# A two-block transformer kernel: the 16 meta tokens' transposes and products cut from 128 to 16 rows and columns, and their memsets removed

## The chip, the core and the metric

The kernel runs on one core of a Trainium2 chip. The core has TensorE (PE, with its weight loads shown apart as PEld), VectorE (DVE), ScalarE (ACT), GpSimd (POOL) and SyncE (SP), which starts DMAs. The engines run side by side and wait for each other through semaphores. The time is that of one execution on the device in microseconds (us); lower is better.

## The reference

Two transformer blocks in float32 are run one after the other, on 512 tokens of width 1024. The first puts 16 learned meta tokens in front (528 tokens) and has two layers: one with differential attention (here stage A) and one with latent attention (stage B), each followed by a gated MLP with a short convolution. The second block has a convolution and windowed attention side by side (stage C) and another MLP. The change touches the attention of the first block alone:

```python
# differential attention (A), 8 heads: q1, q2, k1, k2 64 wide, v 128 wide, L = 528 keys
a = softmax(mask(q1 @ k1.T * 64**-0.5)) - lam * softmax(mask(q2 @ k2.T * 64**-0.5))
o = a @ v
# latent attention (B), 16 heads: q and k 96 wide (64 + 32 rotary), v 64 wide
p = softmax(mask(q @ k.T * 96**-0.5))
o = p @ v
# mask: key chunk <= query chunk; the 16 meta tokens are chunk 0, then chunks of 64
```

## The kernel before, in words

Activations lie with features on the 128 partitions and tokens along the free axis. Weights come in halves of 128 x 1024. ACT makes a rounded copy `w_hi` of each (L1383), POOL the rest `w_lo` (L434), and every linear product is three passes: `w_hi` with `x_hi`, `w_hi` with `x_lo`, `w_lo` with `x_hi` (L455 to L457). The products inside the attention are plain float32.

Each head's queries are done in five units, from the longest to the shortest. A unit `idx` has `t = 4 - idx` blocks of 128 keys behind the 16 meta keys: units 0 to 3 have 128 queries and 16 + 128 t keys, unit 4 has the 16 meta queries and the 16 meta keys (`nq` = 16, t = 0). For a unit the engines do this:

- PE `scores` (L577): queries x keys into PSUM. In A two maps from 64 rows each, on partitions 0 to 63 and 64 to 127; in B one map from 96 rows.
- DVE `maximum` (L997, L999), ACT `exps` (L1473), DVE `combine` (L1010 to L1021): the probabilities in `prob`, queries on partitions, keys along the free axis, the meta keys in columns 0 to 15.
- PE `transposes`: t blocks of 128 keys (L596), then the block that holds the meta keys (L600). L600 transposes columns 0 to 127 of `prob`, of which the first 16 are wanted.
- ACT `take_transposed`: copies the t blocks to `pt` (L1483) and rows 0 to 15 of the meta block to `pt_meta` (L1485).
- PE `values`: t products with `v_tok` (L614) and one with `v_meta` (L616), summed in one PSUM region; stationary are the values (128 wide in A, 64 in B), moving the probabilities. DVE `take_output` (L1028) copies the result away.

`value_transposes` does once per head what `transposes` does for the values: four blocks (L634) and the meta block (L635); ACT copies them (L1491, L1493).

L616 multiplies all 128 rows of `v_meta` and `pt_meta`, of which ACT fills 16. So at the start POOL clears `v_meta`, `pt_meta` and `prob` (L438 to L440) and raises `blocks_clear`, for which PE waits once, ahead of the first value transposes, and ACT once, ahead of the first exponentials.

All orders are written out by hand. In A (`head_a` on PE) a head runs, for each unit: scores of the next unit, transposes of this one, a piece of the next head's projections (24 products in three passes; in unit 3 a second piece follows the values), values of this one; then the next head's value transposes. In B (`head_b`): pieces 0 and 1 of the next head, values 4 of the head before, scores 2, transposes 0, scores 3, piece 2, transposes 1, values 0, scores 4, piece 3, value transposes, values 1, transposes 2, next head's scores 0, values 2, transposes 3, next head's scores 1, values 3, transposes 4. Semaphores count up from unit to unit; PE waits for `a_ready` (combined probabilities), `pt_ready` (ACT's copies), `exp_done`, `qk_ready` (rotated queries and keys) and `o_taken`.

In the built program each product names the part of the 128 x 128 array it takes, rows (contraction) x columns (width of the stationary operand), rounded up to 32, 64 or 128: 64x128 for A's scores, 128x64 for B's values, 128x128 for all else in A and B, B's 96-row scores among it.

Of the kernel before, what the change touches and what calls it, by code (L numbers as in the profile page):

```python
# [31 lines left out]
P = 128  # L32
D = 1024
KD = D // P
META = 16
# [124 lines left out]
def wait(eng, semaphore, value):  # L160

    if not isinstance(value, int) or value > 0:
        eng.wait_ge(semaphore, value)


def program(nc, x_t, stream, params, positions, out):
    tabs_dram = nc.inline_tensor(rotary_tables(), "rotary_tables").ap()
    consts_dram = nc.inline_tensor(shape_constants(), "shape_constants").ap()
    with ExitStack() as ctx:
# [3 lines left out]
        def sem(name):  # L173
            return ctx.enter_context(nc.semaphore(name))
# [20 lines left out]
        ident = cst[:, 0:P]  # L195
        at = [0]

        def carve(n):
            at[0] += n
            assert at[0] <= SCRATCH  # L200
            return scratch[:, at[0] - n:at[0]]
# [4 lines left out]
        vt_buf = carve(T1)  # L206
        v_tok = carve(2 * 512).rearrange("p (a n) -> p a n", a=2)
        v_meta = carve(2 * P).rearrange("p (a n) -> p a n", a=2)
        o_buf = carve(KD * T1).rearrange("p (k t) -> p k t", k=KD)
        prob = carve(4 * T1).rearrange("p (a m t) -> p a m t", a=2, m=2)  # L210
        pt = carve(2 * 512).rearrange("p (a n) -> p a n", a=2)
        pt_meta = carve(2 * P).rearrange("p (a n) -> p a n", a=2)
# [65 lines left out]
        ps = ctx.enter_context(nc.psum_tensor("ps", [P, 8, 512], F32))  # L278
# [24 lines left out]
        g_ready = sem("g_ready")  # L303
        consts_set = sem("consts_set")
        lam_step = sem("lam_step")
        blocks_clear = sem("blocks_clear")
        lam_exp_done = sem("lam_exp_done")
        tabs_made = sem("tabs_made")
        rot_step = sem("rot_step")
# [1 line left out]
        vt_done = sem("vt_done")  # L311
# [70 lines left out]
        def unit(idx):  # L382
            t = 4 - idx
            nq = P if t else META
            return t, nq, (META + P * (t - 1) if t else 0)
# [11 lines left out]
        def prob_of(slot):  # L397
            return prob[:, slot // 2, slot % 2, :]
# [4 lines left out]
        @block.sync  # L403
        def _(sp):
            def load_half(j, i=0):

                wait(sp, lo_ready, j - 3 + 4 * i)
                sp.dma_start(w_raw[:, j % 4, :], stream[j + 4 * i]).then_inc(raw_loaded[j % 4], 16)

            for j in range(4):  # L410
                sp.dma_start(h[:, 2 * j:2 * j + 2, :], x_t[:, 2 * j:2 * j + 2, :]).then_inc(x_loaded[j], 16)
                if j == 0:
                    load_half(0)
            for j in range(1, 4):
                load_half(j)
            with sp.Fori(0, HALVES // 4 - 1) as i:
                for j in range(4, 8):
                    load_half(j, i)
            for j in range(HALVES // 4 * 4, HALVES):
                load_half(j)  # L420
            for m in range(KD):
                sp.wait_ge(fin_ready, m + 1)
                sp.dma_start(out[:, m, :], h[:, m, META:T1]).then_inc(stored, 16)
            sp.wait_ge(stored, 16 * KD)


        @block.gpsimd
        def _(pool):
            def lo_part(j, i=0):
                pool.wait_ge(hi_ready, j + 1 + 4 * i)  # L430
                wait(pool, half_done, j - 3 + 4 * i)
                for c in range(0, HW, HW // LO_CUTS):
                    cols = slice(c, c + HW // LO_CUTS)
                    last = nc.gpsimd.tensor_tensor(w_lo[:, j % 4, cols], w_raw[:, j % 4, cols],  # L434
                                                   w_hi[:, j % 4, cols].bitcast(F32), ALU.subtract)
                last.then_inc(lo_ready, 1)

            nc.gpsimd.memset(v_meta[:, :, :], 0.0)  # L438
            nc.gpsimd.memset(pt_meta[:, :, :], 0.0)
            nc.gpsimd.memset(prob[:, :, :, :], 0.0).then_inc(blocks_clear, 1)  # L440
            for j in range(4):
                lo_part(j)
            with pool.Fori(0, HALVES // 4 - 1) as i:
                for j in range(4, 8):
                    lo_part(j, i)
            for j in range(HALVES // 4 * 4, HALVES):
                lo_part(j)
# [3 lines left out]
        def _(pe):  # L451
# [129 lines left out]
            def transposes(kind, hd, turn, idx, more=True):  # L581

                t, nq, _ = unit(idx)
                u = (5 * hd if kind == "A" else 5 * HEADS_A + 5 * hd) + idx
                pb = prob_of(prob_slot(kind, turn, idx))
                pe.wait_ge(a_ready, u + 1)
                wait(pe, pt_ready, u)
                if kind == "A" and idx == 0:
                    pe.wait_ge(v_ready, hd + 1)
                    wait(pe, o_taken, u)  # L590
                if kind == "B" and idx == 0 and more:
                    pe.wait_ge(kv_taken, 2 * hd + 3)
                if kind == "B" and idx == 2 and more:
                    pe.wait_ge(v_ready, HEADS_A + hd + 2)
                for b in range(t):
                    last = nc.tensor.transpose(ps[:, 6, b * P:b * P + nq],  # L596
                                               pb[0:nq, META + b * P:META + b * P + P], ident[0:nq, 0:nq])
                bank, c = (6, t * P) if t < 4 else (7, 0) if kind == "A" else (1, 384)

                last = nc.tensor.transpose(ps[:, bank, c:c + P], pb[:, 0:P], ident)  # L600
                last.then_inc(t_done, 1)

            def values(kind, hd, turn, idx):

                t, nq, _ = unit(idx)
                u = (5 * hd if kind == "A" else 5 * HEADS_A + 5 * hd) + idx
                up, par_ = (turn + idx) % 2, turn % 2
                pe.wait_ge(pt_ready, u + 1)
                wait(pe, o_taken, u)
                w = P if kind == "A" else 64  # L610
                rows = slice(0, P) if kind == "A" else slice(64 * par_, 64 * par_ + 64)
                o = ps[rows, 7, P:P + nq]
                for b in range(t):
                    nc.tensor.matmul(o, v_tok[:, par_, b * w:b * w + w], pt[:, up, b * P:b * P + nq],  # L614
                                     start=b == 0, stop=False)
                nc.tensor.matmul(o, v_meta[:, par_, 0:w], pt_meta[:, up, 0:nq],  # L616
                                 start=t == 0, stop=True).then_inc(pv_done, 1)

            def value_transposes(kind, hd, par_):

                if kind == "A":
                    pe.wait_ge(chunk_taken, 6 * hd + 6)
                    wait(pe, pt_ready, 5 * hd)
                    wait(pe, o_taken, 5 * hd)
                    meta = ps[:, 7, 0:P]
                else:
                    pe.wait_ge(kv_taken, 2 * hd + 2)
                    if not isinstance(hd, int) or hd:
                        pe.wait_ge(pt_ready, 5 * HEADS_A + 5 * hd - 3)
                    pe.wait_ge(chunk_taken, 6 * HEADS_A + 2 * hd + 1)  # L630
                    meta = ps[:, 0, 384:512]

                for b in range(4):
                    nc.tensor.transpose(ps[:, 6, b * P:b * P + P], vt_buf[:, META + b * P:META + b * P + P], ident)  # L634
                nc.tensor.transpose(meta, vt_buf[:, 0:P], ident).then_inc(vt_done, 1)  # L635

            def sub_sum(n, bank0):

# [58 lines left out]
            for p in range(6):  # L697
                piece_a(0, p)
            scores("A", 0, 0, 0)
            pe.wait_ge(blocks_clear, 1)  # L700
            value_transposes("A", 0, 0)
            head_a(0, 0)
            with pe.Fori(0, (HEADS_A - 2) // 2) as i:
# [38 lines left out]
            for m in range(TILES_C):  # L742
# [4 lines left out]
                if m == 4:  # L747
                    pe.wait_ge(y_ready, 3)
                    for b in range(4):
                        last = nc.tensor.transpose(ps[:, 3, b * P:b * P + P], vt2[:, b * P:b * P + P], ident)  # L750
                    last.then_inc(vt2_done, 1)
                for u in range(8):
# [3 lines left out]
                    if m == s_at + 2:  # L756
                        pe.wait_ge(p2_ready, u + 1)
                        wait(pe, pt2_ready, u)
                        for i in range(4):
                            for kb in range(k0 // P, 2):  # L760
                                last = nc.tensor.transpose(ps[:, 6 + kb, i * P:i * P + P],
                                                           prob2[:, i, kb * P:kb * P + P], ident)
                        last.then_inc(t2_done, 1)
                    if m == s_at + 4:
# [3 lines left out]
                        for kb in range(k0 // P, 2):  # L768
                            last = nc.tensor.matmul(ps[0:64, 1, :], v2[:, n - 1 + kb, g * 64:g * 64 + 64],  # L769
                                                    pt2[:, kb, :], start=kb == k0 // P, stop=kb == 1)  # L770
                        last.then_inc(pv2_done, 1)
                for u in range(8):
                    g, n = divmod(u, 4)
                    k0 = 0 if n else P
                    if m == unit2_at(u):
                        pe.wait_ge(k2q2_ready, 6)
                        wait(pe, masked, u)
                        for i in range(4):
                            e, pair = divmod(i, 2)
                            rows = slice(64 * e, 64 * e + 64)  # L780
                            last = nc.tensor.matmul(ps[:, 4 + e, pair * 256 + k0:pair * 256 + 256],
                                                    q2[rows, 2 * g + pair, n * P:n * P + P],
                                                    k2[rows, g, (n - 1) * P + k0:(n + 1) * P],
                                                    start=True, stop=True)
# [581 lines left out]
        def _(act):  # L1366
# [198 lines left out]
            inverse_rms(N_A, D, T1, r)  # L1565
            for j in range(3, 7):
                hi_part(j)
            act.wait_ge(blocks_clear, 1)
            exps("A", 0, 0, 0)
            take_values("A", 0, 0)  # L1570
            head_a(0, 0, 4)
# [47 lines left out]
            for m in range(TILES_C):  # L1619
# [4 lines left out]
                for u in range(8):  # L1624
# [5 lines left out]
                    if m == unit2_at(u) + 1:  # L1630
                        k0 = 0 if u % 4 else P
                        act.wait_ge(max2_step, 4 * u + 4)
                        for i in range(4):
                            last = A.activation(prob2[:, i, k0:], prob2[:, i, k0:], ACT.Exp, bias=neg2[:, i:i + 1],
                                                accum_out=sum2[:, i:i + 1])
# [150 lines left out]
```

## Time and profile before

| | us |
|---|---|
| median of three runs | 2223.09 |
| lowest, highest run | 2222.1, 2229.47 |
| the profiled execution, time | 2229.47 |
| the profiled execution, span of the core | 2227.3 |

The profile is of one execution. The page gives busy times by engine, the chain of waits that ended last, and groups of instructions by line. A plain float32 product shows as two instructions with a load each, a transpose and a pass of L455 to L457 as one. Matmul rows overlap, because their ends are modelled with a tail: the distance between two starts tells more than a duration. In a row of the timeline the stationary shape (rows*columns) stands ahead of the moving one. A is the stretch up to about 270 us, B that from 768 to 1000 us; between them and behind them stand the MLPs and stage C.

### The profile page before, as it was taken

Reading aid. Unit: us, or ns where it says so; the run is one execution under the profiler, and the core shown is the slowest. Engines: PE = TensorE matmul, PEld = TensorE weight load, DVE = VectorE, ACT = ScalarE, POOL = GpSimd, SP = SyncE. Lnnn points to the kernel's source line nnn. Section 1 sums busy time; section 2 is a strip of 40 time slices with the busy share of each in tenths; the row PEclk is TensorE's granted clock in tenths of the full one; section 3 lists DMA queues with packets and bytes.
Section 4 is the critical chain, followed back from the end, with each engine's and each line's share of the span. In section 5 each row is a group of like instructions: output and inputs, shape, how many; then the busy total and the mean of one; then the engine's idle time right before and its main releaser. Section 6 shows DMA issues by size and latency. Waiting matters only on the chain.

```text
span 2227.3 us, 40390 instructions
## 1 busy us (share of the span) xinstructions
PE 2150.4 (97%) x14044; PEld 1907.1 (86%) x14044; DVE 1138.0 (51%) x2068; ACT 786.1 (35%) x1407; POOL 1113.8 (50%) x1387
## 2 busy tenths in 40 slices
PE   7999899999999899999999999999999999999997
PEld 7888799999999777769999999877778878888886
DVE  6666745334146777763544414775631364425244
ACT  3444524222133355542422313434343224323232
POOL 5444246545556421113655546664455575656553
PEclk9999999999999999989999999999999999999999
DMA  4222122222223201112222222322222232322322
GB/s 172 72 71 75 57 67 98 92 85 94 95 76 114 67 31 36 38 34 76 94 95 85 94 95 86 103 85 76 85 85 95 97 120 86 104 85 94 104 85 76
DMA packets 52502, 188.25 MB, mean 85 GB/s; under 512 B 5824, under 2 KB 5952, under 8 KB 52416
## 3 DMA queue, kind: packets, MB, share of 16 engines
q1 hardware_dynamic: 51408, 185.16, 24.7%
q10 hardware_dynamic: 1008, 1.89, 0.3%
q8 instruction: 60, 0.98, 0.2%
q14 instruction: 26, 0.21, 0.0%
HBM read 184.93 MB, written 2.10 MB: 84 GB/s over the span
## 4 chain that ended last, share of the span: by engine, by line
PE 88%; DVE 8%; ACT 2%; issue 2%; DMA 0%; DVEq 0%; SPq 0%; ACTq 0%
PE ps L455 27%; PE ps L457 26%; PE ps L456 26%; PE ps L577 3%; PE ps L614 2%; PE ps L596 1%; DVE g_lo L822 1%; PE ps L616 1%; DVE g_hi L820 1%; PE ps L769 1%; ACT scratch L1473 1%; PE ps L600 1%; DVE scratch L942 1%; DVE scratch L1021 0%; ACT scratch L1529 0%
## 5 line engine op out<-in xcount | busy, mean ns | idle before, releaser
L434 POOL TENSOR_TENSOR w_lo<-w_raw,w_hi 128x256 fp32r<-128x256 f32 x1380 | 1111.2, 838 | 1088.8 <-ACT w_hi L1383 1088.8
L455 PE MATMUL ps<-x_hi,w_hi 128*128 128x264 f32 (+2 forms) x2760 | 881.2, 319 | 3.9 <-DVE scratch L1348 2.4
L456 PE MATMUL ps<-x_lo,w_hi 128*128 128x264 f32 (+2 forms) x2760 | 868.6, 315 | 0.0
L457 PE MATMUL ps<-x_hi,w_lo 128*128 128x264 f32 (+2 forms) x2760 | 867.5, 314 | 0.0
L455 PEld LDWEIGHTS ps<-x_hi,w_hi 128*128 128x128 f32 x2760 | 522.9, 189 | 47.6 <-issue 7.7
L456 PEld LDWEIGHTS ps<-x_lo,w_hi 128*128 128x128 f32 x2760 | 521.5, 189 | 33.1 <-issue 0.8
L457 PEld LDWEIGHTS ps<-x_hi,w_lo 128*128 128x128 f32 x2760 | 521.5, 189 | 32.3
L1383 ACT ACTIVATE w_hi<-w_raw 128x1024 fp32r<-128x1024 f32 x345 | 361.3, 1051 | 314.5 <-PE ps L457 311.9
L455 PE MATMUL ps<-g_hi,w_hi 128*128 128x264 f32 (+2 forms) x1312 | 409.2, 312 | 15.3 <-DVE g_lo L822 14.5
L456 PE MATMUL ps<-g_lo,w_hi 128*128 128x264 f32 (+2 forms) x1312 | 408.0, 311 | 0.0
L457 PE MATMUL ps<-g_hi,w_lo 128*128 128x264 f32 (+2 forms) x1312 | 407.4, 311 | 0.0
L455 PEld LDWEIGHTS ps<-g_hi,w_hi 128*128 128x128 f32 x1312 | 249.5, 190 | 32.0 <-DVE g_lo L822 17.1
L456 PEld LDWEIGHTS ps<-g_lo,w_hi 128*128 128x128 f32 x1312 | 249.6, 190 | 13.1
L457 PEld LDWEIGHTS ps<-g_hi,w_lo 128*128 128x128 f32 x1312 | 249.6, 190 | 13.0
L833 DVE TENSOR_TENSOR h<-ps,h 128x528 f32 (+2 forms) x80 | 55.9, 699 | 287.4 <-PE ps L457 287.4
L1442 ACT ACTIVATE scratch<-scratch,par 128x528 f32<-128x528 f32 (+2 forms) x66 | 54.3, 822 | 321.3 <-DVE scratch L848 321.3
L848 DVE TENSOR_TENSOR scratch<-ps,r 128x528 f32<-128x528 f32 (+2 forms) x66 | 46.1, 698 | 152.1 <-PE ps L457 136.2
L1473 ACT ACTIVATE scratch<-ps,small 128x400 f32<-128x400 f32 (+4 forms) x160 | 76.6, 481 | 105.5 <-DVE small L999 104.5
L858 DVE TENSOR_TENSOR scratch<-ps,r 128x528 f32<-128x528 f32 (+2 forms) x66 | 46.1, 698 | 129.7 <-PE ps L457 129.7
L577 PE MATMUL ps<-scratch 64*128 64x16 f32 (+9 forms) x384 | 94.0, 419 | 15.5 <-DVE scratch L942 7.2
L822 DVE TENSOR_TENSOR g_lo<-scratch,g_hi 128x528 f32 (+6 forms) x98 | 95.4, 974 | 9.7
L1320 DVE TENSOR_TENSOR scratch<-ps,acc 128x512 f32<-128x512 f32 x47 | 32.4, 690 | 130.4 <-PE ps L457 130.3
(169 smaller groups left out, 1760.0 us busy)
## 6 DMA issues: line engine op xcount, KB each, us to landing
w_raw<-stream SPq DMA_DIRECT2D x345, 512.0 KB, 3.2
h<-x_t SPq DMA_DIRECT2D x4, 528.0 KB, 8.6
out_t<-h SPq DMA_DIRECT2D x8, 256.0 KB, 2.1
scratch<-rotary_tables ACTq DMA_DIRECT2D x4, 264.0 KB, 5.6
par<-params ACTq DMA_DIRECT2D x1, 342.5 KB, 5.2
scratch<-positions ACTq DMA_DIRECT2D x1, 256.0 KB, 2.7
cst<-shape_constants ACTq DMA_DIRECT2D x1, 193.0 KB, 6.6
```

Source lines behind the costliest of these rows:

```text
L434: last = nc.gpsimd.tensor_tensor(w_lo[:, j % 4, cols], w_raw[:, j % 4, cols], w_hi[:, j % 4, cols].bitcast(F32), ALU.subtract)
L455: nc.tensor.matmul(out_ap, w_hi[:, s, c], xh[:, k, cols], start=first, stop=False)
L456: nc.tensor.matmul(out_ap, w_hi[:, s, c], xl[:, k, cols], start=False, stop=False)
L457: return nc.tensor.matmul(out_ap, w_lo[:, s, c], xh[:, k, cols], start=False, stop=last)
L577: last = nc.tensor.matmul(flat[:, b + k0:b + k1], q, k_buf[rows, turn % 2, k0:k1], start=True, stop=True)
L822: V.tensor_tensor(lo, src, hi.bitcast(F32), ALU.subtract).then_inc(ready, 1)
L833: V.tensor_tensor(hm, result(j + m, T), hm, ALU.add).then_inc(tile_taken, 1)
L848: V.tensor_tensor(cut(a_pad[:, 2:2 + T], T), result(j, T), cut(r[:, 0:T], T), ALU.mult).then_inc(tile_taken, 1)
L858: V.tensor_tensor(cut(b_val[:, 0:T], T), result(j + 1, T), cut(r[:, 0:T], T), ALU.mult).then_inc(tile_taken, 1)
L1383: A.activation(w_hi[:, j % 4, :], w_raw[:, j % 4, :], ACT.Copy).then_inc(hi_ready, 1)
L1442: A.activation(conv[:, 0:T], a_pad[:, 0:T], ACT.Identity, bias=par[:, bass.ds(b + 2 * i, 1)], scale=par[:, bass.ds(o + 2 * i, 1)]).then_in ...
L1473: last = A.activation(prob_of(c)[0:nq, 0:nk], flat[0:nq, b:b + nk], ACT.Exp, bias=neg_max[0:nq, c:c + 1], accum_out=sums[0:nq, c:c + 1])
```

## The change

The meta transposes take 16 columns in place of 128 and write 16 partitions; the meta products contract over 16 rows in place of 128. With that nothing reads the rows that the memsets cleared, and they go, with their semaphore and the two waits for it. All other instructions and their order stay.

```diff
--- before.py
+++ after.py
@@ -303,7 +303,6 @@
         g_ready = sem("g_ready")
         consts_set = sem("consts_set")
         lam_step = sem("lam_step")
-        blocks_clear = sem("blocks_clear")
         lam_exp_done = sem("lam_exp_done")
         tabs_made = sem("tabs_made")
         rot_step = sem("rot_step")
@@ -435,9 +434,6 @@
                                                    w_hi[:, j % 4, cols].bitcast(F32), ALU.subtract)
                 last.then_inc(lo_ready, 1)
 
-            nc.gpsimd.memset(v_meta[:, :, :], 0.0)
-            nc.gpsimd.memset(pt_meta[:, :, :], 0.0)
-            nc.gpsimd.memset(prob[:, :, :, :], 0.0).then_inc(blocks_clear, 1)
             for j in range(4):
                 lo_part(j)
             with pool.Fori(0, HALVES // 4 - 1) as i:
@@ -597,7 +593,7 @@
                                                pb[0:nq, META + b * P:META + b * P + P], ident[0:nq, 0:nq])
                 bank, c = (6, t * P) if t < 4 else (7, 0) if kind == "A" else (1, 384)
 
-                last = nc.tensor.transpose(ps[:, bank, c:c + P], pb[:, 0:P], ident)
+                last = nc.tensor.transpose(ps[0:META, bank, c:c + P], pb[:, 0:META], ident)
                 last.then_inc(t_done, 1)
 
             def values(kind, hd, turn, idx):
@@ -613,7 +609,7 @@
                 for b in range(t):
                     nc.tensor.matmul(o, v_tok[:, par_, b * w:b * w + w], pt[:, up, b * P:b * P + nq],
                                      start=b == 0, stop=False)
-                nc.tensor.matmul(o, v_meta[:, par_, 0:w], pt_meta[:, up, 0:nq],
+                nc.tensor.matmul(o, v_meta[0:META, par_, 0:w], pt_meta[0:META, up, 0:nq],
                                  start=t == 0, stop=True).then_inc(pv_done, 1)
 
             def value_transposes(kind, hd, par_):
@@ -622,17 +618,17 @@
                     pe.wait_ge(chunk_taken, 6 * hd + 6)
                     wait(pe, pt_ready, 5 * hd)
                     wait(pe, o_taken, 5 * hd)
-                    meta = ps[:, 7, 0:P]
+                    meta = ps[0:META, 7, 0:P]
                 else:
                     pe.wait_ge(kv_taken, 2 * hd + 2)
                     if not isinstance(hd, int) or hd:
                         pe.wait_ge(pt_ready, 5 * HEADS_A + 5 * hd - 3)
                     pe.wait_ge(chunk_taken, 6 * HEADS_A + 2 * hd + 1)
-                    meta = ps[:, 0, 384:512]
+                    meta = ps[0:META, 0, 384:512]
 
                 for b in range(4):
                     nc.tensor.transpose(ps[:, 6, b * P:b * P + P], vt_buf[:, META + b * P:META + b * P + P], ident)
-                nc.tensor.transpose(meta, vt_buf[:, 0:P], ident).then_inc(vt_done, 1)
+                nc.tensor.transpose(meta, vt_buf[:, 0:META], ident).then_inc(vt_done, 1)
 
             def sub_sum(n, bank0):
 
@@ -697,7 +693,6 @@
             for p in range(6):
                 piece_a(0, p)
             scores("A", 0, 0, 0)
-            pe.wait_ge(blocks_clear, 1)
             value_transposes("A", 0, 0)
             head_a(0, 0)
             with pe.Fori(0, (HEADS_A - 2) // 2) as i:
@@ -1565,7 +1560,6 @@
             inverse_rms(N_A, D, T1, r)
             for j in range(3, 7):
                 hi_part(j)
-            act.wait_ge(blocks_clear, 1)
             exps("A", 0, 0, 0)
             take_values("A", 0, 0)
             head_a(0, 0, 4)
```

The order of PE's instructions is the same in both. In B, unit 1's transposes, unit 0's values and unit 4's scores stand so before (the shape is that of the output; `ps` is PSUM, `cst` holds the identity, `scratch` the probabilities, values, queries and keys):

```order
L596 MATMUL ps<-cst,scratch 128x128 x3
L600 MATMUL ps<-cst,scratch 128x128
L614 MATMUL ps<-scratch 64x128 x4
L616 MATMUL ps<-scratch 64x128
L163 REGISTER_ALU
L577 MATMUL ps<-scratch 128x16
```

and so now:

```order
L592 MATMUL ps<-cst,scratch 128x128 x3
L596 MATMUL ps<-cst,scratch 16x128
L610 MATMUL ps<-scratch 64x128 x4
L612 MATMUL ps<-scratch 64x128
L163 REGISTER_ALU
L573 MATMUL ps<-scratch 128x16
```

Nothing has moved; the lines of the file are shifted by 4, so that L596, L600, L614, L616 and L577 are now L592, L596, L610, L612 and L573, and the meta transpose writes 16 partitions in place of 128. What the output's shape doesn't show: the stationary operand of the meta transpose is now 128x16 (before 128x128), and the meta product contracts 16 rows. The built program gives the meta transposes the part 128x32 of the array, and the meta products 32x128 in A and 32x64 in B.

## Rows read from the trace of the kernel before

**Rows 1.** The page: its first line, and busy time (share) and instructions of each engine

```profile
span 2227.3 us, 40390 instructions
...
PE 2150.4 (97%) x14044; PEld 1907.1 (86%) x14044; DVE 1138.0 (51%) x2068; ACT 786.1 (35%) x1407; POOL 1113.8 (50%) x1387
```

**Rows 2.** The page's chain of waits, shares of the span by engine

```profile
PE 88%; DVE 8%; ACT 2%; issue 2%; DMA 0%; DVEq 0%; SPq 0%; ACTq 0%
```

**Rows 3.** All instructions of L600 and L635: duration ns min/median/max, starts, shapes

```profile
L600 PE MATMUL ps<-cst,scratch x120: 272/273/477, 43.8 to 997.7; 128*128 128x128 f32 x120
...
L635 PE MATMUL ps<-cst,scratch x24: 272/273/273, 38.4 to 976.9; 128*128 128x128 f32 x24
```

**Rows 4.** Stretches from:to: length, busy PE, PEld, DVE, ACT, POOL, clock, DMA

```profile
124.00:152.00 28.00, 26.95 (x214) 24.43 (x213) 19.03 (x52) 11.89 (x35) 12.22 (x16) 1.00 0.23 76
236.00:275.00 39.00, 28.62 (x181) 22.79 (x181) 30.82 (x65) 24.61 (x58) 10.01 (x11) 0.97 0.16 53
840.00:854.00 14.00, 13.30 (x91) 10.27 (x90) 9.90 (x33) 7.46 (x26) 3.04 (x4) 1.00 0.12 38
```

**Rows 5.** PE in order of time in B: start us, us to the last end, line, stationary shape

```profile
857.65 0.49 PE L596 MATMUL ps<-cst,scratch 128*128 128x128 f32 x3
857.97 0.27 PE L600 MATMUL ps<-cst,scratch 128*128 128x128 f32 x1
858.18 1.09 PE L614 MATMUL ps<-scratch 128*64 128x128 f32 x8
859.10 0.38 PE L616 MATMUL ps<-scratch 128*64 128x128 f32 x2
859.41 0.40 PE L577 MATMUL ps<-scratch 96*128 96x16 f32 x2
```

**Rows 6.** PEld (weight loads) in the same stretch

```profile
857.87 0.14 PEld L600 LDWEIGHTS ps<-cst,scratch 128*128 128x128 f32 x1
858.17 0.85 PEld L614 LDWEIGHTS ps<-scratch 128*64 128x64 f32 x8 [0.17 <-issue]
...
859.41 0.30 PEld L577 LDWEIGHTS ps<-scratch 96*128 96x128 f32 x2 [0.17 <-issue]
```

**Rows 7.** PE in order of time in A

```profile
106.74 0.39 PE L616 MATMUL ps<-scratch 128*128 128x128 f32 x2
107.06 0.73 PE L577 MATMUL ps<-scratch 64*128 64x272 f32 x4
```

**Rows 8.** PE in order of time in B: 96 rows behind 128

```profile
851.31 0.27 PE L600 MATMUL ps<-cst,scratch 128*128 128x128 f32 x1
851.42 0.84 PE L577 MATMUL ps<-scratch 96*128 96x400 f32 x2
```

**Rows 9.** POOL in order of time at the start

```profile
1.24 1.86 POOL L440 MEMSET scratch<- 128x2112 f32 x1
8.78 0.93 POOL L434 TENSOR_TENSOR w_lo<-w_raw,w_hi 128x256 fp32r<-128x256 f32 x1 [5.68 <-ACT w_hi L1383]
```

**Rows 10.** What PE waited for in five heads of A: us, times, longest us

```profile
PE ps L634 <- DVE scratch L1028: 2.8, 5, 0.6
PE ps L596 <- DVE scratch L1021: 2.4, 5, 0.5
```

**Rows 11.** PE in order of time in B: two scores that wait

```profile
855.71 0.27 PE L600 MATMUL ps<-cst,scratch 128*128 128x128 f32 x1
856.21 0.51 PE L577 MATMUL ps<-scratch 96*128 96x144 f32 x2 [0.23 <-ACT scratch L1473]
...
862.76 0.27 PE L600 MATMUL ps<-cst,scratch 128*128 128x128 f32 x1
863.51 0.92 PE L577 MATMUL ps<-scratch 96*128 96x16 f32 x3 [0.47 <-DVE scratch L942]
```

**Rows 12.** What PE waited for in fourteen heads of B

```profile
PE ps L577 <- DVE scratch L942: 6.8, 14, 0.7
PE ps L577 <- ACT scratch L1473: 3.0, 13, 0.2
```

## The prediction

> **What bounds the kernel now.** I read the page's busy times first: TensorE is busy for 97% of the span, every other engine for about half [rows 1]. The chain of waits says the same, 88% of it is PE [rows 2]. The memsets of part one of the change are on another engine, so the next question was where the edited TensorE lines run. L600 (the 120 transposes of the 16 meta-token columns) runs from 43.8 to 997.7 us, L635 (its twin for the values, 24 times) from 38.4 to 976.9 [rows 3]. That is two stages: attention A, 8 heads of about 28 us up to 270 us, and attention B, 16 heads of about 14.5 us from 768 to 1000 us. In a steady 28 us of A the matmul rows are busy for 26.95, in 14 us of B for 13.30; in the last A head it is 28.62 of 39 [rows 4]. So time added on TensorE in these stages mostly lands in the total, except where TensorE already waits for somebody. Last I read single rows, since a busy matmul row includes a tail: what counts is the distance from one start to the next.
>
> **What a small product costs.** In B, the transposes L596 (three) start at 857.65 and L600 at 857.97: 0.11 us each [rows 5]. All stream 128 columns, and the weights of L600 load at 857.87, under the last L596 [rows 6]: hidden. Then come products whose stationary operand is 64 columns wide (128*64). The load for the first starts at 858.17, 0.20 us after L600 started where 0.11 is normal [rows 5, 6]. The eight L614 lie 0.109 apart and L616 starts at 859.10, so the first really streams from 859.10 - 8 x 0.109 = 858.23: its load of 0.055 lay open. Leaving that shape costs the same: the second L616 starts 0.11 after the first, at 859.21, and the load of L577 at 859.41, 0.20 again [rows 5, 6]. That load is a plain 128-wide one; the second follows 0.11 later (0.30 for two of 0.19) though only 16 columns stream between them, so it costs 0.11 when open. A shows it for rows: L616 (128*128) twice from 106.74, the second at 106.85, then L577 with 64*128 at 107.06, 0.21 later [rows 7]. Against this, 96 rows after 128 cost nothing: L600 at 851.31, L577 (96*128) at 851.42 [rows 8]; the built program gives both the whole array. My reading: when the part of the array that a product takes changes between whole and half (64 rows or 64 columns), the earlier product runs out first (0.09 us) and the next load lies open: 0.055 for a transpose or 64 columns, 0.11 for 128 plain columns. Sum 0.15 or 0.20 per change of shape.
>
> The Trainium skill, "TensorEngine Tiling (Array Packing)", section "Key Properties", says that changing the tiling mode, not just the tile, drains TensorE; the rows above agree, with their 0.09 us. The same rule speaks against this change.
>
> **The change part by part.** (1) The three memsets and both waits for them. The large one ends at 1.24 + 1.86 = 3.10 us and POOL's first real work starts at 8.78, released by ACT [rows 9]. Worth nothing; the cover is 5.7 us of idle POOL.
>
> (2) The meta transposes L600 and L635: the stationary operand shrinks from 128*128 to 128*16, the moving one stays the 128-column identity. So each still streams for 0.11. The weight load gets shorter, but it is hidden except in the fifth unit of a head, where it comes right behind another shape (0.055 down to an estimated 0.01, so -0.05). The built program gives it a part of the array of 128*32, different from its neighbours', so there is a change of shape on entry and on exit. (3) The meta products L616: 16 rows in place of 128, same columns, so the same stream; part of the array 32*128 (A) or 32*64 (B) where its neighbour L614 has 128*128 or 128*64. One new change on entry; the exit to L577 (A) or L596 (B) was one already.
>
> No row shows a part narrower than 64. Bounds of one such change from the nearest rows: nothing, as 96 against 128 [rows 8], and 0.20 as in [rows 5 to 7]. I take the upper: the half-array rows are the nearer kind. For a load of 16 columns I take 0.01, between 0 and 0.055.
>
> Steady head of A (order: scores, transposes, projection piece, values, five times): enter L600 four times from L596, 4 x 0.10; leave it to a piece five times, 5 x 0.20 = 1.00; enter L616 five times, 1.00; in the fourth unit leave L616 to another piece, 0.20; enter L635, 0.10; fifth L600, -0.05. Sum 2.65. TensorE waits 0.5 us a head for the copy of the fifth output (L1028) ahead of L634, and 0.5 for the combined probabilities (L1021) ahead of L596 [rows 10]. The first wait hides the exit from the fifth L616 (0.15, left out of the sum); the second hides the 0.10 of L635. 2.55 x 7 = 17.9. In the last head TensorE waits anyway [rows 4]: half, 1.2. A: +19.
>
> Steady head of B. Unit 0: L600 in and out to scores, 0.30. But L600 starts at 855.71 and the scores only at 856.21, behind ACT's exponentials, 0.50 where 0.11 is needed [rows 11]: the 0.39 of slack takes it all. Unit 1: L600 in, 0.10 (its exit was a change before); L614 to L616, 0.15. Then L635 0.10, unit 2's L616 is later, unit 1's L616 0.15, unit 2's L600 in and out 0.30: these lie ahead of the next head's first scores, which wait for DVE's rotation from 862.76 + 0.11 to 863.51, 0.64 us [rows 11]; of the 0.55, all is hidden. Left on the path: unit 1's L600 0.10, three L616 (units 0, 2, 3) 0.45, unit 3's L600 0.10 + 0.20, and the fifth unit's L600 -0.05 on entry, +0.20 on exit. Sum 1.00. Both waits recur in every head (14 and 13 times in 14 heads) [rows 12]. 15 heads and a bit: +15.5.
>
> Behind the later transposes stand ACT's copies (L1483, L1485) and behind them the values; the slack there is the score products between, and it does not shrink as long as the delay sits on TensorE itself. DVE is idle for about 30% of both stages and ACT for about half [rows 4], so they follow.
>
> Sum: 19 + 15.5 = 34.5. The profiled execution took 2229.5 (span 2227.3); it would come to 2264. It is the slowest of three, the median is 2223.1, so the forecast is 2223.1 + 34.5 = 2257.6, said as 2258.
>
> **Rivals.** (a) *No waits absorb, or new ones arise.* Without absorption A is 2.8 x 8 = 22.4 and B 1.85 x 16 = 29.6, together 52: 2275. For it: B hands work round between three engines, and a unit that comes later from TensorE delays DVE's next step. Against it: both waits in [rows 11] start from events ahead of the inserted time.
>
> (b) *The narrow transposes stop being transposes.* The transpose is one instruction per block while a plain float32 product is two (L614: eight for four blocks) [rows 5]. If L600 and L635 became plain products, 144 x 0.11 = 16 us more, less what the waits hide (three in each head of B, one in each of A, 56 x 0.11 = 6 us): 34.5 + 10, 2268. The Trainium skill, same page, section "Restrictions", says that column tiling excludes transpose mode for float32 input. No row of before has a transpose on part of the array, so the trace can't tell.
>
> (c) *Only one of the two kinds costs.* The cost may come from rows alone (L616: A 1.2 x 8, B 0.45 x 15, together 16 us, 2239) or from columns alone (the other 18 us, 2241).
>
> (d) *Not slower: no change of shape costs anything* below half the array, because the narrow part lies inside the part its neighbour uses. Then only the shorter open loads remain, 24 fifth units x 0.05 = 1.2 us: 2222. It decides at each exit from L600: if the next load starts 0.11 after L600 it holds. For it: 96 inside 128 [rows 8]. Against it: 64 inside 128 costs 0.09 each way, in every head [rows 5 to 7].
>
> **How the numbers follow.** Forecast with its errors (a change 0.17 to 0.22, absorption a third off) 2247 to 2268: 0.55. (a) 0.13, (b) 0.12, (c) 0.09, (d) 0.08, and 0.03 for something that makes it faster. The range reaches from (c)'s lower case to just past (a): 2238 to 2278, which leaves out (d) and the faster remainder. 0.3%, about what a measurement of this kernel can tell from no change, is 6.7 us: (a), (b), (c) and the forecast are slower, 0.89; (d) is the same, 0.08.
>
> **What will show it.** In the changed profile, in both stages: the next load after an L600 at 0.20 from its start rather than 0.11; L614 to L616 0.20 plus the open load; B's slots behind the fourth L616 0.15 longer. A steady head of A gets 2.5 us longer, one of B 1.0 us (seen from one L635 to the next); waits of L577 in B shrink to near zero. The stages behind 1005 us keep their length. The row for L600 counts 120, or 240 under (b). I am wrong if the heads of A keep their length (d), or if B grows by more than 25 us (a).

## The result, and the profile after

| | before | changed |
|---|---|---|
| median | 2223.80 us (2222.1 to 2229.47, 4 runs) | 2238.51 us (2237.21 to 2241.47, 4 runs) |
| ratio | | 1.0068, 95% interval 1.0053 to 1.0084 |
| profiled execution, span | 2227.3 | 2240.8 |

The change makes the kernel slower by 0.7%, 14.7 us between the medians. The forecast was 2258, +34.5: right in direction, but more than twice too large; that the time lies inside the range (2238 to 2278) is due to its lowest edge, which was set for rival (c). In a second comparison the changed kernel came out at 1.0083 (1.0069 to 1.0097), 18.0 us between the medians.

The page after, first line and busy times, against [rows 1]: TensorE has 17 us more of busy time, its weight loads 7 us less, GpSimd 5 us less; VectorE and ScalarE have what they had.

```profile
span 2240.8 us, 40385 instructions
...
PE 2167.4 (97%) x14044; PEld 1900.3 (85%) x14044; DVE 1139.5 (51%) x2068; ACT 786.5 (35%) x1407; POOL 1108.4 (49%) x1384
```

The same place in B as [rows 5], unit 1's transposes, unit 0's values, unit 4's scores (lines are shifted: L592 and L596 are the transposes, L610 and L612 the value products, L573 the scores):

```profile
863.82 0.49 PE L592 MATMUL ps<-cst,scratch 128*128 128x128 f32 x3
864.15 0.27 PE L596 MATMUL ps<-cst,scratch 128*16 128x128 f32 x1
864.35 1.09 PE L610 MATMUL ps<-scratch 128*64 128x128 f32 x8
865.37 0.43 PE L612 MATMUL ps<-scratch 16*64 16x128 f32 x2
865.72 0.40 PE L573 MATMUL ps<-scratch 96*128 96x16 f32 x2
```

and its weight loads, as [rows 6]:

```profile
864.04 0.09 PEld L596 LDWEIGHTS ps<-cst,scratch 128*16 128x16 f32 x1
864.35 0.85 PEld L610 LDWEIGHTS ps<-scratch 128*64 128x64 f32 x8 [0.22 <-issue]
865.37 0.19 PEld L612 LDWEIGHTS ps<-scratch 16*64 16x64 f32 x2 [0.17 <-issue]
865.72 0.30 PEld L573 LDWEIGHTS ps<-scratch 96*128 96x128 f32 x2 [0.17 <-issue]
```

Two things are to be seen. The meta transpose, now 128*16, starts 864.15 and its load at 864.04, under the last L592: the entry is free. (That the next load comes 0.20 later, at 864.35, is as before, since L610 takes 64 columns.) But between L610 and L612 there is a new hole: the first L610 really streams from 864.40, behind its open load of 0.055, so the eighth starts at 864.40 + 7 x 0.109 = 865.16, and the load of L612 comes only at 865.37, 0.21 later. Before, the load of this product (L616) started under the last L614, at 858.99, before the loads of L614 [rows 6] had ended:

```profile
858.99 0.25 PEld L616 LDWEIGHTS ps<-scratch 128*64 128x64 f32 x2
```

A shows the exit of a narrow transpose to a projection piece, PE and then loads:

```profile
106.20 1.05 PE L610 MATMUL ps<-scratch 128*128 128x128 f32 x8
107.18 0.48 PE L612 MATMUL ps<-scratch 16*128 16x128 f32 x2
107.60 0.73 PE L573 MATMUL ps<-scratch 64*128 64x272 f32 x4
108.26 0.55 PE L592 MATMUL ps<-cst,scratch 128*128 128x128 f32 x3
108.64 0.27 PE L596 MATMUL ps<-cst,scratch 128*16 128x128 f32 x1
```

```profile
107.18 0.29 PEld L612 LDWEIGHTS ps<-scratch 16*128 16x128 f32 x2
...
108.64 0.19 PEld L451 LDWEIGHTS ps<-x_hi,w_hi 128*128 128x128 f32 x1
```

L596 starts at 108.64 and the piece's load (L451) at 108.64, hidden under it. L612 (16*128) again has its load late: the eighth L610 starts at 106.98, the load follows at 107.18, 0.20 later. In the same unit before [rows 7] the eighth L614 started at 106.63 and the load of L616 at 106.63 too:

```profile
106.63 0.30 PEld L616 LDWEIGHTS ps<-scratch 128*128 128x128 f32 x2
```

The waits, to be read against [rows 10] (A) and [rows 12] (B):

```profile
PE ps L592 <- DVE scratch L1016: 2.4, 5, 0.5
PE ps L630 <- DVE scratch L1023: 2.4, 5, 0.5
```

```profile
PE ps L573 <- DVE scratch L937: 5.0, 13, 0.4
PE ps L573 <- ACT scratch L1468: 3.1, 13, 0.2
```

B's wait for DVE fell from 6.8 us (14 times) to 5.0 (13 times), the one for ACT stayed, and A's wait for the output copy fell from 2.8 to 2.4. B's waits absorb little of the 0.85 us a head that I had reckoned for them, since 0.70 of it never came.

Heads by the start of the values' meta transpose (L635, now L631), median of the steady ones, from the starts in each trace; the last two columns are stretches from the first of these starts in the stage to the last (7 heads of A, 15 of B):

| kernel | head of A | head of B | A, first to last | B, first to last |
|---|---|---|---|---|
| before | 28.68 | 14.45 | 205.7 | 216.1 |
| changed | 29.62 | 14.87 | 210.8 | 221.7 |
| difference | +0.94 | +0.42 | +5.1 | +5.6 |

Of the 13.5 us between the two spans, 10.7 lie in these two stretches; between them (last head of A, MLP) it is -1.1, and behind the last head of B +3.9. Most of the last is a lower granted clock and not longer heads. One place shows it: a wait of 2.0 us of TensorE for DVE's `g_lo` in the second MLP, which both kernels have. Stretches around it, before and then changed (length, busy times by engine, granted clock third from the end, DMA share, GB/s):

```profile
1390.00:1400.00 10.00, 8.02 (x67) 7.82 (x66) 6.04 (x9) 4.75 (x5) 5.29 (x7) 1.00 0.20 61
1400.00:1410.00 10.00, 10.00 (x85) 10.00 (x85) 6.97 (x11) 4.40 (x6) 5.59 (x8) 1.00 0.35 113
```

```profile
1400.00:1410.00 10.00, 8.03 (x66) 7.82 (x65) 5.91 (x8) 4.75 (x5) 5.28 (x7) 0.98 0.19 67
1410.00:1420.00 10.00, 10.00 (x73) 10.00 (x73) 5.49 (x10) 3.15 (x5) 5.19 (x8) 0.85 0.30 107
```

TensorE is busy for 8.02 and 8.03 us of the 10 with the wait, and for all of the next 10. Before, the granted clock stays at 1.00; in the changed kernel it is 0.98 and 0.85, that is 0.4 + 3.0 us at 1.2 instead of 2.4 GHz, half of which is lost. Stretches of 20 us show a second such place at 1800 to 1840 in the changed kernel and none before, so some 3.4 of the 3.9 us are lost at these two. The other way round there are 6.8 us at the low level at 40 to 60 us before (granted 0.83), and about half of that in the changed one (0.91); so A's stretch grew by 5.1 and not by the 6.6 that seven heads of +0.94 make.

The medians don't average the clock out either. Each execution has a mean granted clock, as a share of 2.4 GHz. Over 27 runs of the changed kernel it is 0.991 (0.987 to 0.994), over 53 of the kernel before, beside the experiments, 0.993 (0.990 to 0.995). At the same clock the difference is smaller: at 0.993 the changed kernel takes 2237.4 us (mean of 5 runs) and the one before 2224.7 (26 runs), 12.7 us; at 0.992 and 0.991 it is 12.5 and 13.6. So about 13 us belong to the longer heads. What is left of the 14.7 lies within its interval; what is left of the 18.0 goes with the clock, whose mean is 0.989 there against 0.993. The three kernels with 16 rows (this one and two below) have the lower mean in every comparison (0.989 to 0.991), the four with 64 or 96 rows or with narrow transposes alone have 0.993; how the change would bring that about is not shown.

### The profile page after: what moved, and what is told of

It reads as the page before. It is cut to its first block, busy times and chain, and to the rows that moved or that the text cites. A ratio compares the mean times of both kernels' runs of the same rounds, so it can differ in the third digit from the quotient of the medians.

```text
span 2240.8 us, 40385 instructions
## 1 busy us (share of the span) xinstructions
PE 2167.4 (97%) x14044; PEld 1900.3 (85%) x14044; DVE 1139.5 (51%) x2068; ACT 786.5 (35%) x1407; POOL 1108.4 (49%) x1384
## 4 chain that ended last, share of the span: by engine, by line
PE 89%; DVE 7%; ACT 2%; issue 2%; DMA 0%; DVEq 0%; SPq 0%; ACTq 0%
PE ps L451 26%; PE ps L452 26%; PE ps L453 26%; PE ps L573 3%; PE ps L610 2%; PE ps L612 1%; PE ps L592 1%; DVE g_lo L817 1%; DVE g_hi L815 1%; DVE scratch L935 1%; PE ps L764 1%; ACT scratch L1468 1%; PE ps L596 1%; DVE scratch L1016 0%; ACT scratch L1524 0%
## 5 line engine op out<-in xcount | busy, mean ns | idle before, releaser
L451 PE MATMUL ps<-x_hi,w_hi 128*128 128x264 f32 (+2 forms) x2760 | 880.2, 319 | 3.7 <-DVE scratch L1343 2.4
L451 PEld LDWEIGHTS ps<-x_hi,w_hi 128*128 128x128 f32 x2760 | 520.5, 189 | 49.0 <-issue 7.7
L451 PE MATMUL ps<-g_hi,w_hi 128*128 128x264 f32 (+2 forms) x1312 | 409.9, 312 | 15.4 <-DVE g_lo L817 14.6
L451 PEld LDWEIGHTS ps<-g_hi,w_hi 128*128 128x128 f32 x1312 | 249.8, 190 | 32.3 <-DVE g_lo L817 17.1
L573 PE MATMUL ps<-scratch 64*128 64x16 f32 (+9 forms) x384 | 94.1, 420 | 13.9 <-ACT scratch L1468 6.3
```

Source lines behind the costliest of these rows:

```text
L451: nc.tensor.matmul(out_ap, w_hi[:, s, c], xh[:, k, cols], start=first, stop=False)
L573: last = nc.tensor.matmul(flat[:, b + k0:b + k1], q, k_buf[rows, turn % 2, k0:k1], start=True, stop=True)
```

## The experiments

Theory R, formed from the rows above: only the 16-row product costs (a change of the part of the array, the price as predicted), and a transpose never leaves the whole array. (Theory T in the expectations is the part of R on the transposes.) Rivals: P, the prediction's own (both kinds cost, something else gives time back); N, 64 columns is a part of its own and 16 is not; few rows are slow by themselves.

**Rows alone.** Edit on the kernel before:

```diff
-                nc.tensor.matmul(o, v_meta[:, par_, 0:w], pt_meta[:, up, 0:nq],
+                nc.tensor.matmul(o, v_meta[0:META, par_, 0:w], pt_meta[0:META, up, 0:nq],
```

> Of the change only the product with the 16 meta values is made narrow (16 rows in place of 128); meta transposes stay 128 columns wide and the three memsets stay. Theory R (only the change of rows costs, 0.20 us to the next load's start where 0.11 was, plus an open load; a transpose of 16 columns changes nothing): all of the loss is here, 2237 to 2240 against 2223.8 before, heads of A +0.94, heads of B +0.40 us, as in the changed kernel. Rival P (the prediction's: every narrow product, the transposes too, costs, but something else gave time back): this one alone 2232 or less, or its heads shorter than the changed kernel's.

Measured: 2242.63 against 2224.72, ratio 1.0074 (1.0062 to 1.0086), heads 29.66 and 14.91. All of the loss is here (changed: 1.0068 and 1.0083, heads 29.62 and 14.87). The time is above the expected 2237 to 2240; the heads are longer by 0.98 and 0.46 where 0.94 and 0.40 were expected, and the mean granted clock is 0.991 against 0.993.

**Transposes alone.**

```diff
-                last = nc.tensor.transpose(ps[:, bank, c:c + P], pb[:, 0:P], ident)
+                last = nc.tensor.transpose(ps[0:META, bank, c:c + P], pb[:, 0:META], ident)
```

and the same for L635.

> Of the change only the meta transposes are made narrow (16 columns in place of 128); the product keeps 128 rows and the memsets stay. Theory R: no change of length, 2222 to 2225; in the rows the load behind a narrow transpose starts 0.11 us after it, not 0.20; at most 1.2 us gained from the shorter open loads. The prediction's step: +18 us, 2241.

Measured: 2223.90 against 2224.72, ratio 0.9994 (0.9985 to 1.0003), heads 28.61 and 14.40: 0.05 to 0.07 us a head shorter. In A 0.05 of it comes between the fifth unit's L600 and the piece behind it, the shorter open load. The +18 us that the prediction put on the transposes are refuted.

**64 rows in A.**

```diff
+                kr = 64 if kind == "A" else P
-                nc.tensor.matmul(o, v_meta[:, par_, 0:w], pt_meta[:, up, 0:nq],
+                nc.tensor.matmul(o, v_meta[0:kr, par_, 0:w], pt_meta[0:kr, up, 0:nq],
```

> The kernel before with 64 rows in A's meta product (B keeps 128), memsets and transposes as before. Theory R (the price is for the change of the part of the array, not for few rows): the product then takes the same 64 x 128 part as the scores behind it, so in units 0 to 2 the cost only moves from the exit to the entry (entry 0.20 us from start to load, exit to the scores 0.11, where it was 0.11 and 0.20); what is left is unit 3 (0.2 in, 0.2 out) and unit 4's entry, partly hidden: heads of A +0.4 to +0.6 us, in all +3 to +5: 2228. Rival (few rows themselves are slow, or every row-narrow product pays on both sides): heads of A +0.9 as with 16 rows, +8 us: 2232.

Measured: 2227.80, ratio 1.0012 (1.0003 to 1.0021), head of A 29.15 (+0.47 where 16 rows cost +0.94). Its loads in unit 0 (the product is L617):

```profile
106.43 0.18 PEld L617 LDWEIGHTS ps<-scratch 64*128 64x128 f32 x1
106.44 0.18 PEld L577 LDWEIGHTS ps<-scratch 64*128 64x128 f32 x1
```

The first load of L617 at 106.43 comes late, 0.20 behind the start of the eighth L614 at 106.22; but the load of the scores L577 starts at 106.44, next to it, where it waited 0.20 us for the last L616 in [rows 7]. One of the two maps of the scores even runs beside the product (matmuls from 106.43 and 106.44), presumably the one on the other 64 partitions, and the load of the other map, at 106.65, follows the start of the second L617 (106.64) at once. Product and scores share the 64-row part, and the price has moved from exit to entry: from the eighth L614 to the next L596 it is 1.09 us here as before. So what is paid for is the change, not the few rows.

**96 rows.** `v_meta[0:96, ...]`, `pt_meta[0:96, ...]`.

> The kernel before with 96 rows in the meta product of A and B; the built program gives 96 rows the whole array. Memsets and transposes as before. If the price is for the change of the part of the array: no change, 2222 to 2227, the load of the product with 96 rows starts with the last L614. If fewer rows cost by themselves: as with 16 rows, 2240.

Measured: 2226.54 against 2224.36, ratio 1.0005 (0.9996 to 1.0014), heads 28.68 and 14.45 as before. No price. This also speaks against few rows being slow by themselves.

**Transposes of 64 columns.** `pb[:, 0:64]` into `ps[0:64, ...]` in units 0 to 3 (the fifth unit keeps 128 columns), and `vt_buf[:, 0:64]`.

> The kernel before with meta transposes of 64 columns (24 of the values, 96 of the probabilities; the 24 of the fifth units keep 128), a part of the array of 128 x 64 in the built program, the width at which B's value products pay. Memsets and products as before. Theory T (a transpose never leaves the whole array, whatever its width): 2222 to 2226, load behind it 0.11 us after its start. Theory N (64 columns is a part of its own, narrower ones are not): each of the 120 pays 0.15 in and 0.10 to 0.20 out, some hidden in waits: +20 us, 2245.

Measured: 2224.60, ratio 1.0003 (0.9993 to 1.0012), heads 28.68 and 14.45. N falls: at the width at which B's plain products pay, a transpose pays nothing.

**The same 16 columns as a plain product.**

```diff
-                last = nc.tensor.transpose(ps[0:META, bank, c:c + P], pb[:, 0:META], ident)
+                last = nc.tensor.matmul(ps[0:META, bank, c:c + P], pb[:, 0:META], ident, start=True, stop=True)
```

and the same for L635.

> The meta transposes with 16 columns as plain float32 products with the identity, not as transposes: same operands, same result, two instructions each in place of one. Memsets stay, value products as before. Both theories pay the second instruction, 144 x 0.11 = 16 us less about 6 hidden: 2234. Theory T adds the changes of shape, as they are now plain products of 16 columns: rows show the load behind them at 0.20 us from the second one's start, and 0.20 in: +18 more, 2250 to 2254. Theory N: load at 0.11, 2232 to 2236.

Measured: 2254.67, ratio 1.0136 (1.0120 to 1.0151), +30 us; heads 30.90 and 15.50. PE and loads in B, the place of [rows 5]:

```profile
862.74 0.49 PE L596 MATMUL ps<-cst,scratch 128*128 128x128 f32 x3
863.16 0.39 PE L600 MATMUL ps<-cst,scratch 128*16 128x128 f32 x2
863.49 0.76 PE L614 MATMUL ps<-scratch 128*64 128x128 f32 x5
```

```profile
863.16 0.11 PEld L600 LDWEIGHTS ps<-cst,scratch 128*16 128x16 f32 x2 [0.17 <-issue]
863.48 0.63 PEld L614 LDWEIGHTS ps<-scratch 128*64 128x64 f32 x6 [0.21 <-issue]
```

The third L596 starts at 862.96, the load of L600 at 863.16, 0.20 later; its second instruction starts at 863.28, and the load of L614 follows at 863.48. So R holds with its numbers: the same operands pay on both sides as a plain product, and nothing as a transpose. The gap of 0.20 is what the prediction put on L600; the second instruction comes on top. 2250 to 2254 was expected.

**Memsets put back** into the changed kernel, with both waits.

> The changed kernel with the three memsets and the two waits for them put back (the narrow transposes and products stay). All theories here: POOL has 5.7 us of idle behind the memsets, so the same time as the changed kernel, within 2 us. If the memsets mattered (start delayed, or POOL and DVE in each other's way), it is 2 us or more slower.

> The changed kernel itself, next to the two below, for a comparison on one chip: 1.006 to 1.008 of before.

Measured on one chip: with memsets 2241.31, ratio 1.0073 (1.0060 to 1.0087); without 2243.49, 1.0083 (1.0069 to 1.0097). No gain from leaving them out: the intervals overlap, and the heads are equal (29.62 and 29.64, 14.87 and 14.87).

**The other way: B's values 128 wide.** The edit in `values`, lines between left out (the product with `v_meta` is widened in the same way, and `take_values` shifts the values by 64 columns for odd heads):

```diff
-                o = ps[rows, 7, P:P + nq]
+                o = ps[:, 7, P:P + nq]
...
-                    nc.tensor.matmul(o, v_tok[:, par_, b * w:b * w + w], pt[:, up, b * P:b * P + nq],
+                    nc.tensor.matmul(o, v_tok[:, par_, b * w:b * w + P], pt[:, up, b * P:b * P + nq],
```

> The other way round: B's value products (stationary 64 columns wide before) are made 128 wide, so that nothing in B leaves the whole array. The second 64 output rows are not used; for odd heads the values lie 64 columns further on, so that the window of 128 puts them into rows 64 to 127. Everything else as before. Theory R: ten changes of shape per head of B go, each 0.15 or 0.20 us, 1.6 us a head; those ahead of TensorE's two waits (0.35 ahead of unit 3's scores, 0.29 ahead of the next head's first scores) only make the waits longer; left 0.9 us x 16 = 15: 2209. Rival W (B is bound by the round trips through DVE and ACT, waits take it all): 2222 to 2224, with PE's waits in B grown from 10 us to about 30.

Measured: 2216.74, ratio 0.9958 (0.9945 to 0.9971), -8 us where R said -15; head of B 13.91, -0.54. The waits in fourteen heads of B:

```profile
PE ps L577 <- DVE scratch L941: 13.5, 14, 1.0
PE ps L577 <- ACT scratch L1472: 6.2, 14, 0.6
```

They were 6.8 and 3.0 us [rows 12] and are 13.5 and 6.2: 0.7 us a head more. The direction is R's, and W, the waits, took a good part. R reckoned 1.6 us a head, of which the two waits would take 0.64; they took 0.71, 0.54 came out as gain, and where the remaining 0.35 went is not shown.

**Wide everywhere.** The wide values, the windowed attention's eight value products 128 wide too, narrow transposes, the memset of `prob` left out; the meta product keeps 128 rows.

> The wide values of B (whole array), and the same in the windowed attention of the second block (eight value products of 64 columns made 128 wide; of the output the half that belongs to the group is read), with the change's narrow meta transposes, without the memset of the probabilities. The meta product keeps 128 rows. Theory R: 8 us less than before from B as measured, and in the windowed attention two changes of shape less for each of eight units, 0.15 + 0.20 us, 2.7 us; narrow transposes 0 to 1: 2213. Rival: the windowed part waits for others there: 2216, as with B alone.

Measured: 2215.19, ratio 0.9956 (0.9943 to 0.9970). It beats both kernels, but can't be told from the wide values alone; the 2.7 us expected of the windowed part are not shown.

**Wide and swapped.** The kernel "wide everywhere" with unit 2's values ahead of the next head's first scores.

```diff
+                step(values, 2)
                 if more:
                     scores("B", hd + 1, (turn + 1) % 4, 0)
-                step(values, 2), step(transposes, 3)
+                step(transposes, 3)
```

> The wide kernel (B and windowed attention) with one step of B moved on PE: unit 2's values ahead of the next head's first scores, which wait 1.0 us per head for DVE's rotation there. Values 2 take 0.65 us and need ACT's copy of transposes 2, about 0.9 us behind them; so most of them fits into that wait. If so: PE's wait of the scores for L941 falls from about 1.0 us a head to under 0.5, the head of B gets 0.3 us shorter, 2210. Rival: the wait only changes its name (values wait for ACT's copy L1483, and the later scores hold DVE up): 2214 to 2217.

Measured: 2235.92, ratio 1.0050 (1.0037 to 1.0064), 20 us worse than without the swap. Both expectations miss it. A head of B takes 14.75 us for 13.90 without the swap, 13 us in all; the rest goes with the clock (0.987 to 0.992 for 0.992 and 0.993; the two runs at 0.992 are 12.9 us apart). PE's waits in fourteen heads:

```profile
PE ps L612 <- DVE scratch L1027: 23.8, 13, 1.9
PE ps L576 <- ACT scratch L1472: 5.6, 13, 0.4
```

L612 (values 2) now waits 1.8 us a head for L1027, DVE's copy of values 1: there is one output region in PSUM, and DVE's copy stands behind its own rotation (L941) and combination (L1013). I had looked only at ACT's copy of the transposes.

## Why the prediction was off

The step that failed is part (2): "there is a change of shape on entry and on exit" of the meta transposes. It was priced with the upper of two bounds, the nearer rows being plain products of 64 columns, and the built program names a part of 128x32 for it. The chip runs a float32 transpose of 16 or 64 columns without a change. By the prediction's own terms that was 1.45 us of 2.65 in a head of A (entries 0.40, exits 1.00, L635 0.10, less 0.05) and 0.55 of 1.00 in a head of B, in all 18 of the 34.5 us. With the transposes alone nothing of it appeared: 0.9994, heads of A and B 0.07 and 0.05 shorter. What happened is one half of its rival (c), rows alone, 2239; both halves together had 0.09.

The rest stood up:

- The price of a change is right: start to load 0.20 where 0.11 was, plus an open load. Three units of A, last L614 to the scores' load: 0.43 before, 0.62 after, +0.19 (said 0.20). Unit 3 with its second exit +0.39 (said 0.40).
- A came to 0.94, not to the 1.20 of the products less 0.05. By the medians of the steady heads units 0 to 2 give 0.19, 0.20 and 0.13, unit 3 0.39, the fifth unit's entry 0.08 of its 0.20, and its shorter load takes 0.05 back. So two entries were put too high. In the fifth unit, from the last pass of the piece to the load of the value transposes, it was 0.95 before and is mostly 1.04 after: before, DVE copied the fifth output only at the end of its own part of the piece (L953), and the first 0.1 us of TensorE's delay fits in there; I had taken the copy to follow TensorE at once. In unit 2 the 0.06 went between the piece and the end of the value products, where before a load of L614 had stood open for 0.08.
- B's products came to 0.46 for 0.45 (rows alone), 0.42 with the shorter load of the transposes.
- Together 0.94 x 7 + 0.42 x 16 = 13.3 us, for 12.5 to 13.6 between runs at the same granted clock. That the median of 2238.5 falls on the 2239 of (c) is partly luck: its 16 us for the products were too high, and the lower clock made up for it.
- The memsets are worth nothing, as said [rows 9].
- Rival (b) is refuted: L596 still counts one instruction per transpose (120 in the whole trace, x1 in the rows above). The sentence of the Trainium skill, "TensorEngine Tiling (Array Packing)", section "Restrictions", that column tiling excludes transpose mode for float32, did not apply as I used it: the transposes stay transposes and nothing drains around them, as if no column tiling were in force, although the built program names a part of 128x32. Why, no run here shows.
- Rival (d), contained parts are free, is refuted for plain products by the 16 rows (1.0074) and the 16 columns (1.0136).

So the fault was to take the price of an operation without a row of its own from another kind of operation, and to give (c), which needs only that one of the two kinds is free, 0.09.

## What to carry to other kernels

Cutting a plain product to the rows or columns that matter saved nothing here, since the moving side stays as long, and cost 0.15 to 0.20 us each time TensorE had to change between parts of its array; padding a narrow operand with zeros or leftovers to the full 128 can be the faster form, as B's values show (0.9958). Before narrowing, list the shapes in program order and count the changes, transposes left out. And when a step is moved into a wait, look at every semaphore it waits for, the output region's too.

## What the runs showed of the hardware

- A float32 transpose of 16 or 64 stationary columns between full-width products costs no change (0.9994 and 1.0003), the same 16 columns as a plain product cost 0.20 us from start to load on both sides (1.0136).
- 96 rows count as the whole array (1.0005); 64 rows share a part with other 64-row products: in the run with 64 rows the scores' first load starts 0.01 us behind the product's (106.43 and 106.44), and the two run side by side.
- A change from 32 to 64 rows costs as much as one from 128: in A the second L612 (16*128) starts at 107.40, by 107.18 + 0.11 + 0.11, and the load of the scores (64*128) at 107.60.
- The same 2.0 us wait was followed by 3.4 us at the low clock in one execution and by none in another. From run to run of the changed kernel the mean granted clock goes from 0.994 to 0.987 and the time from 2237.2 to 2248.0 us.
